# Sample keys turned by VectorE in 32x32 blocks, and sample scores in 16 tiles of the PE array, in a hybrid decoder layer

## The chip, the cores and the metric

The kernel runs on one core of a Trainium2 chip. Its five engines are TensorE (PE, with its weight loads PEld), VectorE (DVE), ScalarE (ACT), GpSimd (POOL) and SyncE (SP, here only a queue for DMAs). The metric is the time of one execution on the device in microseconds (us). Less is better.

## The reference, cut to what matters

One decoder layer takes a prompt of 256 tokens and 8 sample requests of 8 tokens each (64 sample rows, so 320 token columns). One projection `w_in` makes q, k, v, gates, indexer inputs and pool inputs for all of them, and `w_out` mixes the two branches back. The change touches one step of branch A, the attention of the sample requests. Each request has 8 pages of 128 cached keys and values, found through a page table, and 8 new keys:

```python
k_sel = jnp.where(in_past, cache_k[phys, row], gather_rows(k_new, ns).astype(cache_k.dtype))
qg = q.reshape(B, T, N_KV_HEADS, R, D)
logits = jnp.einsum('btgrd,btkgd->btgrk', qg, k_sel, preferred_element_type=F32) * (D ** -0.5)
bias = rel_bias[bucket].astype(F32).reshape(B, T, K, N_KV_HEADS, R)
logits = logits + jnp.transpose(bias, (0, 1, 3, 4, 2))
p = jax.nn.softmax(logits, axis=-1)
o = jnp.einsum('btgrk,btkgd->btgrd', p.astype(v_sel.dtype), v_sel)
```

There are 16 heads in 4 key groups of width 128. The kernel doesn't gather the chosen keys: it scores all 1032 keys of a request (1024 cached, 8 new) and adds a mask that leaves the chosen ones. A request's queries are 128 columns, 32 for each key group.

## The kernel before, in words

The program is a chain of segments over the columns of the projections: `qi`, `qkv`, `q`, `u`, `gb`, `ga`, `out`. Each takes its weights in chunks of 4 x 128 rows by 256 columns (512 KB). For each chunk SP issues the load (`load_chunk`), ACT copies it rounded into `hi` (`hi_chunk`), DVE makes the rest `lo` (`lo_chunk`), and PE runs 24 products of 320 columns each (`products`). There are four slots: ACT may write the slot of chunk c once PE has used chunk c - 4, and ACT and DVE work three chunks ahead of PE. Sixteen chunks are a quad, and after each half of a quad DVE empties two PSUM banks.

The other work is woven between the chunks. In the segment `ga` (4 quads, 64 chunks) it is the sample attention: request `b` takes 8 chunks, and `s` counts them. `pe_weave`, `act_weave` and `dve_weave` give what each engine does after its chunk `s`:

- s = 1 and 2: PE turns the 8 key pages in 32 transposes of 128x128 (L1397) into PSUM; ACT and DVE copy four pages each into `KTs` (`turned_keys`, L1444 and L1438). At s = 2 DVE copies the 8 new keys and the request's queries `qb` (L1465, L1466); ahead of the copies it waits for `e_in`, the load of all sample queries `qS` from DRAM, which ACT issues at the start of the segment (L1845).
- s = 3: PE computes the scores in 12 matmuls (L1406), each of 128 rows by 32 columns of the array, with up to 512 keys moving; `e_s` says that they are done. DVE adds bias and mask (L1470), adds the scaled scores (L1473) and takes the maximum (L1475).
- s = 4: ACT takes the exponential (L1447). s = 5: PE turns the weights of the keys (9 transposes, L1413), ACT copies them.
- s = 6: PE multiplies with the values (36 matmuls, L1423), DVE scales the result into `oN` (L1483). s = 7: PE turns `oN` (L1429), ACT stores it in `qS`.

In a weave the engine's own chunk work stands first: what DVE does after its chunk j comes behind `lo_chunk` of chunk j + 3, and all engines take their instructions in the order written.

GpSimd issues the page loads in its own queue (`on_gpsimd`, L1768). For each further request `b` it waits until the key pages of the one before are turned (`e_kt`), loads 8 key pages of 256 KB (`load_pages`, a page-table read and a DMA each), waits for the transposes of s = 5 and loads the mask, waits for the values' matmuls and loads 8 value pages. The first request's keys are loaded much earlier (`ahead`), the first mask and values at the start of the segment.

## Time and profile before

| | |
|---|---|
| time, median of 3 runs | 2105.53 us (2102.64 to 2108.89) |
| the profiled execution's own time | 2103.51 us |
| its span | 2101.9 us |
| PE busy | 2085.8 us (99% of the span) |
| DVE busy | 1165.2 us (55%) |
| ACT busy | 743.4 us (35%) |
| POOL busy | 409.2 us (19%) |
| mean DMA rate | 193 GB/s |

The page splits the span into 40 slices; PE stands at 9 tenths in all but the last, and the granted TensorE clock at full speed. The segment `ga` lies from about 1324 us to 1623 us of the span, where slices 26 to 32 show the highest DMA rates (240 to 256 GB/s). Times in the rows are microseconds from the span's start. An fp32 matmul of the program appears as two instructions: the 12 score matmuls of a request are 24 in its row.

### The profile page before, as it was taken

The page shows a single profiled execution, that of the slowest core. Times are in us where ns is not written, and L with a number is a line of the kernel's source. Part 1 is how long each engine was busy: PE and PEld are TensorE (multiplying, and loading weights), DVE is VectorE, ACT ScalarE, POOL GpSimd, SP SyncE. Part 2 cuts the span into 40 slices and gives each one's busy share as a digit, 9 for nine tenths or more (in the row PEclk, how much of TensorE's full clock was granted, in tenths as well). Part 3 has the DMA queues.
Part 4 walks back from the last instruction along what each step waited for, and adds up shares of the span by engine and source line. Part 5 has one row for each costly group of instructions (what it writes and reads, how often), then busy time and mean ns, then how long its engine had stood idle before and what let it go on. Part 6 is the DMA issues. An engine that isn't in the chain of part 4 may idle for free. (4 is left out here: it accounts for less than half of the span.)

```text
span 2101.9 us, 38946 instructions
## 1 busy us (share of the span) xinstructions
PE 2085.8 (99%) x14337; PEld 1991.3 (95%) x14337; DVE 1165.2 (55%) x1409; ACT 743.4 (35%) x925; POOL 409.2 (19%) x574
## 2 busy tenths in 40 slices
PE   9999999999999999999999999999999999999997
PEld 7888888999999999999999999999999999999997
DVE  5544544455555445566776767565665744444444
ACT  6433333323332333333333323333334433333333
POOL 1101000011110010235642102222222411111100
PEclk9999999999999999999999999999999999999999
DMA  8777776755554565666666657878787755555454
GB/s 232 210 220 212 224 205 204 221 153 160 147 164 127 179 191 173 181 194 170 196 199 194 189 152 220 255 241 256 244 255 250 240 166 161 163 164 160 152 156 145
DMA packets 341328, 406.01 MB, mean 193 GB/s; under 512 B 20332, under 2 KB 316204, under 8 KB 341000
## 3 DMA queue, kind: packets, MB, share of 16 engines
q1 hardware_dynamic: 293704, 291.75, 47.6%
q0 software_dynamic: 29968, 94.61, 14.5%
q10 hardware_dynamic: 17584, 18.70, 2.7%
q8 instruction: 44, 0.72, 0.1%
q14 instruction: 28, 0.23, 0.0%
HBM read 377.68 MB, written 31.45 MB: 195 GB/s over the span
## 5 line engine op out<-in xcount | busy, mean ns | idle before, releaser
L245 DVE TENSOR_TENSOR lo<-raw,hi 128x1024 fp32r<-128x1024 f32 x542 | 693.3, 1283 | 665.9 <-ACT hi L240 665.6
L269 PE MATMUL bank<-XX,hi 128*128 128x320 f32 x3264 | 1029.1, 315 | 0.2 <-DVE XX L1619 0.2
L271 PE MATMUL bank<-XX,lo 128*128 128x320 f32 x3264 | 1008.7, 309 | 0.0
L270 PE MATMUL bank<-XX,hi 128*128 128x320 f32 x3264 | 1008.3, 309 | 0.0
L240 ACT ACTIVATE hi<-raw 128x1024 fp32r<-128x1024 f32 x542 | 569.9, 1057 | 866.4 <-PE bank L271 533.9
L269 PEld LDWEIGHTS bank<-XX,hi 128*128 128x128 f32 x3264 | 613.0, 188 | 8.9 <-issue 5.0
L270 PEld LDWEIGHTS bank<-XX,hi 128*128 128x128 f32 x3264 | 613.2, 188 | 2.1
L271 PEld LDWEIGHTS bank<-XX,lo 128*128 128x128 f32 x3264 | 612.6, 188 | 0.0
L256 PE MATMUL bank<-XX,hi 128*128 128x512 f32 x1024 | 355.9, 392 | 0.0
L257 PE MATMUL bank<-XX,lo 128*128 128x256 f32 x1024 | 286.8, 280 | 0.0
L256 PEld LDWEIGHTS bank<-XX,hi 128*128 128x128 f32 x1024 | 191.5, 187 | 42.5 <-issue 0.2
L257 PEld LDWEIGHTS bank<-XX,lo 128*128 128x128 f32 x1024 | 193.5, 189 | 0.0
L1829 POOL TENSOR_TENSOR ends<-ends 128x512 f32 (+1 forms) x16 | 26.1, 1648 | 352.4 <-ACT ends L1571 334.8
L540 POOL DMA_DIRECT2D biasP<-biasD x16 | 8.6, 537 | 272.0 <-PE bank L257 272.0
L824 ACT ACTIVATE relu<-wide 128x384 f32<-128x384 f32 (+1 forms) x32 | 14.0, 438 | 119.5 <-PE wide L786 86.4
L377 DVE TENSOR_TENSOR stg<-bank,rstdB 128x320 f32<-128x320 f32 x72 | 32.0, 486 | 40.0 <-PE bank L271 40.0
L729 POOL DMA_DIRECT2D ipg<-cache_idx_k x64 | 34.7, 542 | 99.6 <-issue 99.6
L1758 POOL DMA_DIRECT2D deck<-cache_k x64 | 34.5, 539 | 92.9 <-issue 92.9
L1072 POOL DMA_DIRECT2D oT<-ohT x16 | 8.8, 551 | 184.8 <-ACT ohT L1266 184.1
L1306 DVE MAX8 tops<-scS 64x8 f32<-64x1032 f32 x32 | 39.1, 1222 | 0.0
L1308 DVE MATCH_REPLACE8 scS<-tops,scS 64x1032 f32<-64x1032 f32 x32 | 38.7, 1209 | 0.0
L1238 PE MATMUL wide<-dl,wp 128*128 128x320 f32 x128 | 37.0, 432 | 0.0
(298 smaller groups left out, 1534.1 us busy)
## 6 DMA issues: line engine op xcount, KB each, us to landing
raw<-w_in SPq DMA_DIRECT2D x416, 512.0 KB, 3.9
raw<-w_out SPq DMA_DIRECT2D x128, 512.0 KB, 3.7
deck<-cache_k POOLq DMA_DIRECT2D x64, 256.0 KB, 4.4
projT<-stg ACTq DMA_DIRECT2D x35, 320.0 KB, 2.9
keep<-cache_v POOLq DMA_DIRECT2D x40, 256.0 KB, 3.5
deck<-cache_v POOLq DMA_DIRECT2D x24, 256.0 KB, 3.7
deck<-maskD POOLq DMA_DIRECT2D x8, 516.0 KB, 5.7
ipg<-cache_idx_k POOLq DMA_DIRECT2D x64, 64.0 KB, 2.6
```

What stands on the lines that cost most here:

```text
L240: nc.scalar.activation(dst, raw[:, slot, :, 0:width], ACT.Copy).then_inc(hi_ready, 1)
L245: nc.vector.tensor_tensor(low, raw[:, slot, :, 0:width], high.bitcast(F32), ALU.subtract).then_inc(lo_ready, 1)
L256: nc.tensor.matmul(both, wh, XX[:, k, :, FREE:N], start=first, stop=False)
L257: mm = nc.tensor.matmul(bank[banks[n]][:, LATE:2 * LATE], wl, XX[:, k, 0, FREE:N], start=False, stop=last)
L269: nc.tensor.matmul(sums, wh, XH[:, k, :], start=first, stop=False)
L270: nc.tensor.matmul(sums, wh, XL[:, k, :], start=False, stop=False)
L271: mm = nc.tensor.matmul(sums, wl, XH[:, k, :], start=False, stop=last)
L729: pool.dma_start(ipg[:, p, :], tile_rows(t["cache_idx_k"][0], page)).then_inc(s_ipg, 16)
L1238: mm = nc.tensor.matmul(sbank[3][:, 0:N], wp[:, a, dt * P:(dt + 1) * P], dl[:, a, :], start=a == 0, stop=a == 3)
L1306: nc.vector.max(tops[:], scS[:]).then_inc(ts_step, 1)
L1308: nc.vector.match_replace(scS[:], tops[:], scS[:], TAKEN).then_inc(ts_step, 1)
L1758: pool.dma_start(dst[p], tile_rows(src, page)).then_inc(landed, 16)
```

## The change

Key pages. A page is now loaded in rows of 32: its 128 keys lie in 32 partitions with 4 keys in each. Two pages share a quarter of the partitions, so the same 2 MB fill the same buffer in another arrangement. DVE turns each of the 8 slots of that buffer with one 32x32-block transpose of 128 x 512 elements (`turned_pages`) straight into `KX`. The 32 transposes on PE and the 8 copies by ACT and DVE are gone. DVE turns the pages of request b + 1 in three shares, during s = 4, 5 and 6 of request b, and those of request 0 after the first three chunks of the segment. The first share waits for all 8 pages.

Scores. They come from 64 matmuls on 32 rows by 32 columns of the array with 256 keys moving, 16 tiles of the array in turn, each summed over four pieces of the head width, and 4 small matmuls for the new keys. Each row tile writes its own PSUM bank, and DVE adds the scores in two instructions instead of one.

Queries. Every row tile needs the queries of its 32 rows of the head width in its own partitions, so `qb` goes to DRAM once (`store_q`, 64 KB) and is read back four times into `qB` (`load_q`, 4 DMAs of 64 KB). GpSimd issues these: `store_q` after the first four key pages, `load_q` after the last four, ahead of the mask. `store_q` waits for `e_kn`, the copy of the queries, which DVE now makes at s = 4 of the request before (`new_keys`). For request 0 the copies and their wait for `e_in` stand after the first chunk.

```diff
             def pe_weave(pe, q, j):
                 u, s = j // 8, j % 8
                 b = q * BQ + u
-                if s in (1, 2):
-                    for p in range(4 * s - 4, 4 * s):
...
-                        for g in range(G):
-                            tr = nc.tensor.transpose(sbank[p % 4][:, g * P:(g + 1) * P], kpg[:, p, g * P:(g + 1) * P], ident[:])
-                        tr.then_inc(e_kt, 1)
                 if s == 3:
...
+                    pe.wait_ge(e_ptA, b)
+                    pe.wait_ge(e_o, b)
                     pe.wait_ge(e_kn, b * 2 + 2)
-                    for c in range(0, LS, 512):
-                        z = min(LS, c + 512)
-                        for g in range(G):
-                            mm = nc.tensor.matmul(wide[32 * g:32 * g + 32, c:z], qb[:, 32 * g:32 * g + 32], KTs[:, g, c:z],
-                                                  start=True, stop=True, skip_group_check=True)
+                    pe.wait_ge(e_kt, b * PAGES + PAGES)
+                    pe.wait_ge(e_qB, b * 64 + 64)
+                    alone(pe)
+                    for c in range(4):
+                        for a in range(4):
+                            for g in range(G):
+                                rows, quarter = slice(32 * a, 32 * a + 32), slice(32 * g, 32 * g + 32)
+                                nc.tensor.matmul(sbank[a][quarter, 0:PAST // 4], qB[rows, c, quarter],
+                                                 KX[rows, 4 * g + c, :, :].rearrange("p n k -> p (n k)"),
+                                                 start=c == 0, stop=c == 3, skip_group_check=True)
+                    for g in range(G):
+                        quarter = slice(32 * g, 32 * g + 32)
+                        mm = nc.tensor.matmul(sbank[0][quarter, PAST // 4:PAST // 4 + T_S], qb[:, quarter], KN[:, g, :],
+                                              start=True, stop=True, skip_group_check=True)
                     mm.then_inc(e_s, 1)
...
+            def turned_pages(dve, b, pages):
+
+                for p in pages:
+                    if p == 0:
+                        dve.wait_ge(e_k, b * (16 * PAGES) + 16 * PAGES)
+                        dve.wait_ge(e_s, b)
...
+                    nc.vector.transpose(KX[:, :, p, :], kpg[:, p, :].rearrange("p (b k) -> p b k", k=32)).then_inc(e_kt, 1)
+
+            def new_keys(dve, b):
+                dve.wait_ge(e_s, b)
+                nc.vector.tensor_copy(KN, kT[:, :, ds(b * T_S + T_P, T_S)]).then_inc(e_kn, 1)
+                nc.vector.tensor_copy(qb.rearrange("p (h n) -> p h n", h=H), qS[:, :, ds(b * T_S, T_S)]).then_inc(e_kn, 1)
...
+            SHARES = (range(0, 3), range(3, 6), range(6, PAGES))
+
+            def dve_weave(dve, q, j, first=False, last=False):
...
+                if first and j < 3:
+                    if j == 0:
+                        dve.wait_ge(e_in, 16)
+                        new_keys(dve, 0)
+                    turned_pages(dve, 0, SHARES[j])
+                if s == 4 and not (last and u):
+                    new_keys(dve, b + 1)
+                if s in (4, 5, 6) and not (last and u):
+                    turned_pages(dve, b + 1, SHARES[s - 4])
...
+                    if dst is keys:
+                        rows = rows.rearrange("(j k) n -> k j n", k=32)
+                    pool.dma_start(dst[p], rows).then_inc(landed, 16)
+
+            keys = [kpg[16 * (p - p % 2):16 * (p - p % 2) + 32, 4 * (p % 2):4 * (p % 2) + 4, :] for p in range(PAGES)]
...
+                def store_q(b):
+                    pool.wait_ge(e_kn, b * 2 + 2)
+                    alone(pool)
+                    pool.dma_start(tile_rows(qD, b), qb).then_inc(e_qD, 16)
+
+                def load_q(b):
+                    pool.wait_ge(e_qD, b * 16 + 16)
+                    alone(pool)
+                    for a in range(4):
+                        src = qD[ds(b, 1)].rearrange("o (c p) n -> p (o c) n", p=32)
+                        pool.dma_start(qB[32 * a:32 * a + 32, :, :], src).then_inc(e_qB, 16)
...
                 load_mask(0)
-                load_pages(pool, 0, "cache_v", vpg, e_v, PAGES // 2)
+                store_q(0)
+                load_pages(pool, 0, "cache_v", vpg, e_v, PAGES // 2, PAGES - 2)
+                load_q(0)
+                load_pages(pool, 0, "cache_v", vpg, e_v, PAGES - 2)
                 load_vnew(0)
                 with pool.Fori(1, NB_S) as b:
                     pool.wait_ge(e_kt, b * PAGES)
                     alone(pool)
-                    load_pages(pool, b, "cache_k", keys, e_k)
+                    load_pages(pool, b, "cache_k", keys, e_k, 0, PAGES // 2)
+                    store_q(b)
+                    load_pages(pool, b, "cache_k", keys, e_k, PAGES // 2)
+                    load_q(b)
                     pool.wait_ge(e_pt, b)
                     alone(pool)
                     load_mask(b)
```

On DVE, in one request of the segment. In the rows `lo` is the chunk work, `deck` holds the logits and keys, `wide` is PSUM and `keep` holds queries and `oN`. Before, from the new keys of a request to its `oN`:

```order
L1465 COPY deck<-keep 128x4x8
L1466 COPY keep<-keep 128x128
L245 TENSOR_TENSOR lo<-raw,hi 128x1024
L1470 TENSOR_TENSOR deck<-deck 128x1032
L1473 SCALAR_TENSOR_TENSOR deck<-wide,deck 128x1032
L1475 TENSOR_REDUCE st<-deck 128x1
L245 TENSOR_TENSOR lo<-raw,hi 128x1024 x2
L1478 RECIPROCAL st<-st 128x1
L245 TENSOR_TENSOR lo<-raw,hi 128x1024
L1483 TENSOR_SCALAR keep<-wide,st 128x128
```

Now, from the maximum of a request to its `oN`:

```order
L1487 TENSOR_REDUCE st<-deck 128x1
L246 TENSOR_TENSOR lo<-raw,hi 128x1024
L1442 COPY deck<-keep 128x32
L1443 COPY keep<-keep 128x128
L1438 STREAM_TRANSPOSE deck<-deck 128x16x32 x3
L246 TENSOR_TENSOR lo<-raw,hi 128x1024
L1438 STREAM_TRANSPOSE deck<-deck 128x16x32 x3
L1490 RECIPROCAL st<-st 128x1
L246 TENSOR_TENSOR lo<-raw,hi 128x1024
L1438 STREAM_TRANSPOSE deck<-deck 128x16x32 x2
L1495 TENSOR_SCALAR keep<-wide,st 128x128
```

The copies for the next request and its eight transposes now stand between the maximum and the `oN` of this one.

On GpSimd, at the end of a request's key pages in the loop (`deck<-cache_k` is a key page, `keep<-cache_v` a value page, an ISA row is a wait or a register move). Before:

```order
L1757 TENSOR_LOAD ptab
L1757 ISA x2
L1758 ISA
L1758 DMA deck<-cache_k 128x512
L1771 ISA
L1771 DMA deck<-maskD 128x1x1032
L1757 TENSOR_LOAD ptab
L1757 ISA x2
L1758 ISA
L1758 DMA keep<-cache_v 128x512
```

Now, at the fourth page, and then behind the eighth:

```order
L1773 DMA deck<-cache_k 32x4x512
L1789 ISA
L1791 ISA
L1791 DMA qD<-keep 128x128
L1769 ISA
L1769 TENSOR_LOAD ptab
L1769 ISA x2
L1773 ISA
L1773 DMA deck<-cache_k 32x4x512
...
L1794 ISA
L1798 DMA keep<-qD 32x4x128 x4
L1786 ISA
L1786 DMA deck<-maskD 128x1x1032
```

The store of the queries, with its wait, stands in the middle of the key pages, and four loads stand ahead of the mask.

## Rows read from the trace of the kernel before

**Rows 1.** Windows view: us; PE, PEld, DVE, ACT, POOL busy (instructions); clock, DMA share, GB/s.

```profile
1420.00:1457.00 37.00, 37.00 (x330) 34.96 (x329) 22.37 (x24) 13.77 (x18) 9.29 (x18) 1.00 0.77 248
```

**Rows 2.** Timeline of PE, one request, product rows between: start us, us, instructions.

```profile
1369.85 1.91 PE L1397 MATMUL wide<-ident,deck 128*128 128x128 f32 x16
1371.51 0.39 PE L269 MATMUL bank<-XX,hi 128*128 128x320 f32 x1
...
1382.38 0.41 PE L269 MATMUL bank<-XX,hi 128*128 128x320 f32 x1
...
1394.12 1.30 PE L1423 MATMUL wide<-keep,deck 128*32 128x128 f32 x40
...
1396.35 0.41 PE L269 MATMUL bank<-XX,hi 128*128 128x320 f32 x1
1399.97 0.27 PE L1429 MATMUL wide<-ident,keep 128*128 128x128 f32 x1
...
1417.86 1.97 PE L1406 MATMUL wide<-deck,keep 128*32 128x512 f32 x24
1426.90 1.14 PE L1413 MATMUL wide<-ident,deck 128*128 128x128 f32 x9
```

**Rows 3.** Timeline of DVE in the same stretch.

```profile
1396.55 0.35 DVE L1483 TENSOR_SCALAR keep<-wide,st 128x128 f32<-128x128 f32 x1 [2.46 <-PE wide L1423]
...
1412.14 1.28 DVE L1438 COPY deck<-wide 128x512 f32<-128x512 f32 x2
...
1419.99 1.23 DVE L1473 SCALAR_TENSOR_TENSOR deck<-wide,deck 128x1032 f32<-128x1032 f32 x1 [1.74 <-PE wide L1406]
1421.26 1.23 DVE L1475 TENSOR_REDUCE st<-deck 128x1 f32<-128x1032 f32 x1
1422.40 1.22 DVE L245 TENSOR_TENSOR lo<-raw,hi 128x1024 fp32r<-128x1024 f32 x1
```

**Rows 4.** Timeline of GpSimd in the same stretch.

```profile
1417.14 0.54 POOL L1758 DMA_DIRECT2D deck<-cache_k  x1 [0.79 <-issue]
1418.38 0.54 POOL L1758 DMA_DIRECT2D deck<-cache_k  x1 [0.70 <-issue]
...
1428.79 0.54 POOL L1771 DMA_DIRECT2D deck<-maskD  x1 [3.70 <-PE wide L1413]
```

**Rows 5.** DMA issues (count, KB each, median us to landing): segment ga, then whole span.

```profile
deck<-cache_k POOLq DMA_DIRECT2D x48, 256.0 KB, 4.2
...
oT<-ohT POOLq DMA_DIRECT2D x16, 128.0 KB, 2.2
keep<-projT ACTq DMA_DIRECT2D x1, 512.0 KB, 10.1
```

**Rows 6.** All page loads of L1758: time to landing, min/median/max.

```profile
DMA to landing us min/median/max: 2.8/4.1/7.8
```

**Rows 7.** Timelines of ACT, DVE and PE in the first request.

```profile
1332.50 0.41 ACTq L1845 DMA_DIRECT2D keep<-projT  x1
...
1334.27 2.36 DVE L245 TENSOR_TENSOR lo<-raw,hi 128x1024 fp32r<-128x1024 f32 x2 [2.57 <-ACT hi L240]
...
1342.78 0.18 DVE L1465 COPY deck<-keep 128x32 f32 x1 [2.62 <-DMA keep<-projT]
1342.92 0.23 DVE L1466 COPY keep<-keep 128x128 f32 x1
...
1343.20 1.97 PE L1406 MATMUL wide<-deck,keep 128*32 128x512 f32 x24 [0.87 <-DVE keep L1466]
...
1345.10 0.41 PE L269 MATMUL bank<-XX,hi 128*128 128x320 f32 x1
```

**Rows 8.** Windows view at the span's start and end, and PE's last busy window.

```profile
15.00:20.00 5.00, 5.00 (x32) 4.63 (x32) 1.61 (x4) 2.28 (x6) 2.10 (x4) 0.81 1.04 332
...
2091.00:2094.00 3.00, 0.89 (x8) 0.63 (x6) 1.17 (x5) 0.80 (x3) 0.00 (x0) 1.00 0.57 222
2094.00:2096.00 2.00, 0.00 (x0) 0.00 (x0) 1.95 (x5) 1.16 (x2) 0.00 (x0) 0.90 0.03 7
```

More of the change, by code:

```diff
@@ L112, in hybrid_layer @@
     maskD = dram("maskD", (N_S, LS))
+    qD = dram("qD", (NB_S, P, H * T_S))
     biasD = dram("biasD", (H, VEC))
@@ L154, in hybrid_layer @@
         ptab = sb("ptab", [1, NB_S * PAGES], I32)
-        keep = sb("keep", [P, G * N + (LS + 1) // 2 + L2 + L2 // 2 + 3 * KVW + POOLW // P * NB_S * STATE])
+        keep = sb("keep", [P, G * N + 4 * H * T_S + L2 + L2 // 2 + 3 * KVW + POOLW // P * NB_S * STATE])
         at = [0]
@@ L423, in hybrid_layer @@
         gated_a, exped_a = sem("gated_a"), sem("exped_a")
-        (e_in, e_rel, e_k, e_v, e_mask, e_masked, e_vnew, e_kt, e_kcA, e_kcD, e_kn, e_s, e_lg, e_mx, e_exp, e_ri, e_pt,
+        (e_in, e_rel, e_k, e_v, e_mask, e_masked, e_vnew, e_kt, e_qD, e_qB, e_kn, e_s, e_lg, e_mx, e_exp, e_ri, e_pt,
          e_ptA, e_pv, e_on, e_ot, e_o) = (sem(n) for n in (
-             "e_in", "e_rel", "e_k", "e_v", "e_mask", "e_masked", "e_vnew", "e_kt", "e_kcA", "e_kcD", "e_kn", "e_s", "e_lg",
+             "e_in", "e_rel", "e_k", "e_v", "e_mask", "e_masked", "e_vnew", "e_kt", "e_qD", "e_qB", "e_kn", "e_s", "e_lg",
              "e_mx", "e_exp", "e_ri", "e_pt", "e_ptA", "e_pv", "e_on", "e_ot", "e_o"))
@@ L1429, in pe_weave @@
                     nc.tensor.transpose(sbank[3][:, P:2 * P], oN, ident[:]).then_inc(e_ot, 1)
-            def turned_keys(eng, copy, s, b, even, done):
-                eng.wait_ge(e_s, b)
-                eng.wait_ge(w_pe, 4 * NG)
-                eng.wait_ge(ut_out, 16 * NG * (NB_S + 1))
-                for p in range(4 * s - 4 + (0 if even else 1), 4 * s, 2):
-                    eng.wait_ge(e_kt, b * PAGES + (p + 1))
-                    copy(KTs[:, :, p * P:(p + 1) * P], sbank[p % 4].rearrange("p (g n) -> p g n", g=G)).then_inc(done, 1)
+            def turned_pages(dve, b, pages):
[3 more added lines that the diff above has]
+                        dve.wait_ge(e_s, b)
+                        dve.wait_ge(w_pe, 4 * NG)
+                        dve.wait_ge(ut_out, 16 * NG * (NB_S + 1))
+                    nc.vector.transpose(KX[:, :, p, :], kpg[:, p, :].rearrange("p (b k) -> p b k", k=32)).then_inc(e_kt, 1)
[3 more added lines that the diff above has]
+                nc.vector.tensor_copy(qb.rearrange("p (h n) -> p h n", h=H), qS[:, :, ds(b * T_S, T_S)]).then_inc(e_kn, 1)
             def act_weave(act, q, j):
@@ L1442, in act_weave @@
                 b = q * BQ + u
-                if s in (1, 2):
-                    turned_keys(act, lambda o, i: nc.scalar.activation(o, i, ACT.Copy), s, b, True, e_kcA)
                 if s == 4:
@@ L1757, in load_pages @@
                     page = pool.value_load(ptab[0:1, ds(b * PAGES + p, 1)], min_val=0, max_val=N_PHYS - 1)
-                    pool.dma_start(dst[p], tile_rows(src, page)).then_inc(landed, 16)
-            keys = [kpg[:, p, :] for p in range(PAGES)]
+                    rows = tile_rows(src, page)
+                    if dst is keys:
+                        rows = rows.rearrange("(j k) n -> k j n", k=32)
+                    pool.dma_start(dst[p], rows).then_inc(landed, 16)
+            keys = [kpg[16 * (p - p % 2):16 * (p - p % 2) + 32, 4 * (p % 2):4 * (p % 2) + 4, :] for p in range(PAGES)]
             def ahead(pool):
@@ L1860, in on_vector @@
             def on_vector(dve):
-                with dve.Fori(0, NQ - 1) as q:
+                dve_quad(dve, "ga", 0, lambda eng, q, j: dve_weave(eng, q, j, first=True), gate=gate)
+                with dve.Fori(1, NQ - 1) as q:
                     dve_quad(dve, "ga", q, dve_weave, gate=gate)
-                dve_quad(dve, "ga", NQ - 1, then_mix(dve_weave, dve_mix), gate=gate, open_end=True)
+                dve_quad(dve, "ga", NQ - 1, then_mix(lambda eng, q, j: dve_weave(eng, q, j, last=True), dve_mix), gate=gate,
+                         open_end=True)
                 dve_quad(dve, "out", 0, mix_weave(dve_mix, dve_gating), turned=f_t, first=True)
```

39 lines of the change are left out of this document (14 added, 25 removed).

## The prediction, made before the changed kernel ran

> **What bounds the kernel now.** I read the busy shares first, then the windows of the segment `ga`, where the change sits. A window as long as one request has PE busy in all of its 37.00 us at full clock, and DVE in 22.37 [rows 1]. So PE sets the pace here, and what the change takes from PE is a gain as long as nobody makes PE wait. Next comes PE's timeline, to see where a request's time goes. From the first score matmul of one request to that of the next there are 37.4 us: the scores give way to products at 1382.38, `oN` is turned 17.6 us later at 1399.97, and the next scores start at 1417.86, 17.9 us after that; the scores themselves take 1.9 us (1343.20 to 1345.10) [rows 2, 7]. Last I read the timelines of DVE and GpSimd, for what each does between the scores and `oN` [rows 3, 4], since the order puts new work there.
>
> **PE: what goes and what comes.** Sixteen transposes take 1.66 us (1369.85 to 1371.51) [rows 2]; a request has two such sets, so 3.3 us go. The 17.9 us from `oN` to the next scores become 14.6.
>
> The scores are new in form, and no row shows row tiles at work. Before, 24 instructions (two for each of 12 fp32 matmuls) took 1.9 us. Now there are 136. The multiplications are the same: 16 tiles of 32x32 fill the array as the four of 128x32 did. If the array is the limit, they take 1.9 us again. But each instruction is only 256 columns long and shares the array with 15 others. The nearest row in count is the product with the values: 36 matmuls, 72 instructions, from 1394.12 to 1396.35, which is 2.23 us or 31 ns each [rows 2]. At that rate 128 instructions take 4.0 us. The upper end is that row tiles don't overlap: four times the array time, 4 x 1.7 = 6.8 us. I take 3.8, near the row of 31 ns. So PE alone would need 37.4 - 3.3 - 1.9 + 3.8 = 36.0 us for a request, a gain of 1.4 us.
>
> [...]
>
> **The loop through DVE and GpSimd.** This is the part that decides. I count from the moment when the scores of request b end (1419.76 in the stretch of [rows 2 to 4], since they started at 1417.86), as time 0.
>
> - DVE adds scores at 0.23, for 1.23 us; a second small add, 0.2; then the maximum, 1.23; then `lo` of a chunk, which adds 1.15 (starts 1422.40, ends 1423.62, overlapping a little) [rows 3]. That is 4.0.
> - DVE copies the new keys and queries of request b + 1: 0.37 us (1342.78 to 1343.15) [rows 7]. That is 4.4, and only now does `e_kn` let GpSimd go on.
> - GpSimd stands at `store_q`, with four key pages still to issue behind it. Between a release and its DMA lie 0.75 us (PE's transposes end at 1428.04, the mask's DMA starts at 1428.79) [rows 2, 4]. The store starts at 5.15 and ends at 5.69. The first page follows after 0.70, and pages follow each other by 1.24 (1417.14, 1418.38) [rows 4]. So the eighth page is issued at 6.4 + 3 x 1.24 = 10.1.
> - It lands 4.2 us later [rows 5], at 14.3. All key pages lie between 2.8 and 7.8 [rows 6]. Before, this landing had most of a request to happen in. Now DVE waits for it in its queue, with two more `lo`, five more transposes and `oN` behind it.
> - Eight block transposes of 512 elements. No row shows one. Two copies of the same size from PSUM take 1.28 us [rows 3], so 0.6 each from start to start. A cheaper end is 0.4, the dearer end is twice the copy, 1.2. I take 0.6.
> - Three transposes 1.9, `lo` 1.15, a reciprocal 0.15, three transposes 1.8, `lo` 1.15, two transposes 1.25, `oN` 0.35: 7.75 us. So `oN` is there at 22.1.
>
> [...]
>
> PE reaches its wait for `oN` at 17.6. It stands still for 4.5 us. The chunk that PE needs next was made lo at 17.4, so this is one wait and not two. Then come 14.6 us and the scores, 3.8: the period is 22.1 + 14.6 + 3.8 = 40.5 us against 37.4. Seven periods lie between the scores of the first and the last request: 7 x 3.1 = +22 us. Behind the last request nothing is turned, and PE's way to the end is as before.
>
> Everything else that is off PE is covered while the loop holds. ACT's four copies go and were hidden. DVE loses four copies of 0.6 and gets eight transposes of 0.6, within 14 us of idle time per request [rows 1]. The four loads of `load_q` follow the key pages and are wanted some 20 us later; the mask behind them has until the next scores.
>
> **The first request.** In `new_keys` of request 0 DVE waits for `e_in` after the first chunk, with `lo` of the next chunk behind it. ACT issues that load at 1332.50 and it takes 10.1 us; DVE could copy at 1342.78. It had been idle for 2.6 us then, with its other work done [rows 5, 7]. Now DVE stands from 1335.5 on. Meanwhile GpSimd stands at `store_q` too, so fewer pages compete with this load: I let it land at 1339.5 (ends: 1337, 1342.6). Then: copies 1340, store issued 1341, two value pages to 1343.7, four loads of queries to 1346, landing 3.5 to 4.2 later, 1349.7. The pages are turned by 1347.3 (8 x 0.6, two `lo`, copies). PE comes at 1339 and waits for 10 us. The scores end near 1349.7 + 3.8 + 1.7 = 1355, where the 1.7 is the clock, below. Before, products followed at 1345.10 [rows 7]. That is +10 us.
>
> **The clock.** At the end of the span PE is last busy between 2091 and 2094 and the clock is at its lower level for a fifth of 2094 to 2096 (mean 0.90), so it fell near 2095.6, after less than 4 us of idleness or so. At the start, PE was busy in all of 15 to 20, yet the mean is 0.81: 1.9 of 5 us at the lower level [rows 8]. [...] I put in 1 us on each of 7 waits: +7.
>
> **Sum.** 2103.5 (the profiled execution) + 10 + 22 + 7 = 2142.5. That execution is 2 us under the median of the runs, so beside them 2143.
>
> **The rivals.**
> - The loop closes in time, PE keeps the bound. For it: landings as short as 2.8, transposes at 0.4, together 3 us less in the chain, and scores at the array's limit. Then the wait is 1.5 us without a change of clock, the period 35.6 (19.1 + 14.6 + 1.9), seven times -1.8, with +6 at the start: 2097. Against it: three good ends at once. With transposes and landings good and the scores at 2.7 the period is 36.4, and the time about 2103.5 - 7 + 7 = 2104. The faster side starts where `oN` comes before 19.5 and the scores take under 2.5 us. Chance 0.08 for the faster end, 0.05 for the case that comes out as no change.
> - Row tiles don't overlap: the scores take 6.8 us. For it: no row shows the overlap. Eight times +3: 2167. Chance 0.12. If nothing overlapped at all, 64 x 0.43 = 27 us each, 2330; chance 0.02.
> - Block transposes cost 1.2 us. Then +4.8 in each chain, seven times, plus 3: 2180. Chance 0.08.
> - Weights run late. DMA share is 0.77 and 248 GB/s in the segment [rows 1]. Against it: a longer period lowers the rate. As the whole effect it would have PE waiting for `lo` and not for `oN`. It adds 5 to 15 us in 0.05.
> - Forecast: the loop. Chance 0.60.
>
> A difference under 0.3%, 6 us, can't be told from none. Slower 0.87, within 0.05, faster 0.08. The range for 8 in 10 is 2112 to 2175: the lower end is landings of 2.8, transposes of 0.5 and scores near 3, the upper end the rows of tiles that don't overlap with the clock low after each wait.
>
> **What would show it.** Right: after the scores of requests 0 to 6, DVE's first transpose idle for 8 to 10 us on a DMA of `cache_k`; the first of these about 14 us after the scores; PE's L1428 idle for 3 to 6 us on DVE; a clock under 1.00 in these windows; PE's scores near 3.8 us; in the first request DVE's copy idle on `keep<-projT` and PE's first score matmul idle for about 10 us. Wrong: PE busy in all of a request's window (then PE kept the bound), score bursts of 1.9 or 6.8 us, or transposes far from 0.6 us. If the last four key pages were issued before the copy of the queries, the whole loop would be misread.

## The result and the profile after

The changed kernel takes 2161.48 us (median of four runs, 2159.49 to 2163.63) against 2107.21 for the kernel before (2102.64 to 2109.61) on the same chip. The ratio is 1.0261, with a 95% interval of 1.0240 to 1.0281: slower. The forecast was 2143 us with a range of 2112 to 2175. The direction and the range held, and 18 us were missing from the sum. For the profiled execution by itself the sum was 2142.5 and 2163.63 us came out: 21.1 missing.

Two rows of the profile page after, the queue of instructions (packets, MB, share) and the costliest groups:

```profile
q8 instruction: 65, 1.06, 0.2%
...
L1438 DVE STREAM_TRANSPOSE deck<-deck 128x512 f32<-128x512 f32 x64 | 40.7, 683 | 71.4 <-DMA deck<-cache_k 71.4
```

DVE waits 71.4 us for key pages ahead of its new transposes. And the queue that the page calls "instruction" moved 65 packets, which I read as code brought to the engines. The page of before has 44 there. That difference belongs to a third of the loss, as the experiments show.

PE's waits inside `ga` (1320 to 1700 us), as us in total, times, longest:

```profile
PE wide L1428 <- DVE keep L1495: 28.3, 7, 4.9
PE wide L1400 <- DMA keep<-qD: 12.0, 1, 12.0
PE bank L270 <- issue: 11.4, 2, 5.8
PE bank L271 <- issue: 8.4, 2, 5.1
```

The first row is the loop through DVE and GpSimd, in seven of the eight requests. The second is the first request. The other two were in no part of the forecast: PE stands at a product (L270, then L271) for which nothing that the profile shows had to be waited for.

Windows of three successive requests, each from one end of scores to the next, then short windows around two of the waits (columns as in [rows 1]):

```profile
1396.30:1447.10 50.80, 37.58 (x416) 35.28 (x411) 24.75 (x29) 11.57 (x14) 12.74 (x23) 0.87 0.64 194
1447.10:1489.10 42.00, 37.98 (x416) 35.54 (x411) 24.33 (x29) 11.46 (x14) 12.71 (x23) 0.92 0.81 226
1489.10:1542.00 52.90, 38.19 (x411) 35.89 (x411) 24.76 (x29) 11.57 (x14) 12.59 (x23) 0.84 0.64 186
1418.00:1424.00 6.00, 0.33 (x1) 0.14 (x1) 5.16 (x7) 0.90 (x2) 2.73 (x5) 0.58 1.05 345
...
1468.00:1473.00 5.00, 4.68 (x18) 4.68 (x19) 3.09 (x6) 1.85 (x3) 2.14 (x4) 0.50 1.01 357
```

A request was 37.00 us of busy PE at clock 1.00 in [rows 1]. Now most requests take 41 to 42 us, and two take 50.8 and 52.9. The last row is the stretch right after a wait of 3.5 us: PE is busy in 4.68 of 5 us, and the granted clock is 0.50. That is the lower of the two levels, 1.00 and 0.50, at which the clock stands in all the traces here; a mean between them is a window that holds both.

PE's timeline shows where the long requests differ from the others:

```profile
1351.16 4.00 PE L1400 MATMUL wide<-deck,keep 32*32 32x256 f32 x128 [11.98 <-DMA keep<-qD]
...
1418.44 0.33 PE L1428 MATMUL wide<-ident,keep 128*128 128x128 f32 x1 [4.41 <-DVE keep L1495]
...
1424.35 0.63 PE L270 MATMUL bank<-XX,hi 128*128 128x320 f32 x1 [5.58 <-issue]
...
1428.21 0.42 PE L271 MATMUL bank<-XX,hi 128*128 128x320 f32 x1 [3.23 <-issue]
...
1444.20 2.76 PE L1400 MATMUL wide<-deck,keep 32*32 32x256 f32 x128
1446.89 0.25 PE L1405 MATMUL wide<-deck,keep 128*32 128x8 f32 x8
...
1468.32 0.47 PE L1428 MATMUL wide<-ident,keep 128*128 128x128 f32 x1 [3.49 <-DVE keep L1495]
...
1516.65 0.63 PE L270 MATMUL bank<-XX,hi 128*128 128x320 f32 x1 [5.78 <-issue]
...
1522.43 0.43 PE L271 MATMUL bank<-XX,hi 128*128 128x320 f32 x1 [5.15 <-issue]
```

Both "issue" pairs stand at the first products of a quad, where the loop over quads on PE jumps back. Four quads make the segment, and the loop body is the code of one quad with its two requests. It jumps back twice, into the second and the third quad; the last one is written out behind the loop.

The same request on DVE, answering to [rows 3]:

```profile
1447.28 1.22 DVE L1483 SCALAR_TENSOR_TENSOR deck<-wide,deck 128x1024 f32<-128x1024 f32 x1 [3.03 <-PE wide L1405]
...
1450.97 0.22 DVE L1443 COPY keep<-keep 128x128 f32 x1
...
1460.84 1.90 DVE L1438 STREAM_TRANSPOSE deck<-deck 128x512 f32<-128x512 f32 x3 [9.64 <-DMA deck<-cache_k]
...
1467.96 0.31 DVE L1495 TENSOR_SCALAR keep<-wide,st 128x128 f32<-128x128 f32 x1
```

And on GpSimd, answering to [rows 4]:

```profile
1452.01 0.56 POOL L1791 DMA_DIRECT2D qD<-keep  x1 [24.05 <-DVE keep L1443]
...
1457.12 0.55 POOL L1773 DMA_DIRECT2D deck<-cache_k  x1 [0.72 <-issue]
```

The chain is the one of the forecast. The scores end at 1447.14. DVE copies the queries at 1450.97, GpSimd issues the store at 1452.01 after standing for 24.05 us, and the eighth page follows at 1457.12. DVE's first transpose begins at 1460.84, 13.7 us after the scores (forecast 14.3). `oN` is ready 21.1 us after them, and PE turns it at 21.2 (forecast 22.1).

**The account.** The profiled spans differ by 2162.1 - 2101.9 = 60.2 us. The first request gives 10.2 of it (its scores end at 1355.3 instead of 1345.1). The seven periods between ends of scores were 41.0, 50.8, 42.0, 52.9, 41.1, 42.0 and 41.2. The seven before run from 1343.20 [rows 7] to the start of the last request's scores:

```profile
1604.22 1.97 PE L1406 MATMUL wide<-deck,keep 128*32 128x512 f32 x24
```

That is 261.0 us, or 37.3 (37.29) each; the 37.4 of [rows 2] was the longest. The five periods without a jump have a mean of 41.46, which is 4.17 more: 7 x 4.17 = 29.2. The two with a jump have 9.3 and 11.4 on top: 20.7. Together that is 60.1.

### The profile page after: what moved, and what is told of

The parts are those of the page before. It is cut to its first block and busy times, and to the rows that moved or that the text cites. A ratio compares the mean times of both kernels' runs of the same rounds, so it can differ in the third digit from the quotient of the medians.

```text
span 2162.1 us, 40238 instructions
## 1 busy us (share of the span) xinstructions
PE 2084.9 (96%) x14977; PEld 1989.6 (92%) x14977; DVE 1181.3 (55%) x1449; ACT 726.2 (34%) x893; POOL 433.5 (20%) x614
## 5 line engine op out<-in xcount | busy, mean ns | idle before, releaser
L270 PE MATMUL bank<-XX,hi 128*128 128x320 f32 x3264 | 1035.1, 317 | 12.3 <-issue 11.4
L271 PE MATMUL bank<-XX,hi 128*128 128x320 f32 x3264 | 1014.7, 311 | 8.4 <-issue 8.4
L270 PEld LDWEIGHTS bank<-XX,hi 128*128 128x128 f32 x3264 | 619.1, 190 | 21.8 <-issue 16.8
L271 PEld LDWEIGHTS bank<-XX,hi 128*128 128x128 f32 x3264 | 619.1, 190 | 2.1
L1438 DVE STREAM_TRANSPOSE deck<-deck 128x512 f32<-128x512 f32 x64 | 40.7, 683 | 71.4 <-DMA deck<-cache_k 71.4
L730 POOL DMA_DIRECT2D ipg<-cache_idx_k x64 | 34.7, 542 | 99.6 <-issue 99.6
```

The lines of the kernel that those rows point to most:

```text
L270: nc.tensor.matmul(sums, wh, XH[:, k, :], start=first, stop=False)
L271: nc.tensor.matmul(sums, wh, XL[:, k, :], start=False, stop=False)
L730: pool.dma_start(ipg[:, p, :], tile_rows(t["cache_idx_k"][0], page)).then_inc(s_ipg, 16)
L1438: nc.vector.transpose(KX[:, :, p, :], kpg[:, p, :].rearrange("p (b k) -> p b k", k=32)).then_inc(e_kt, 1)
```

## The experiments

The question was what the two gaps at the jumps are, and whether the loop through DVE is really what the other waits come from. My first theory made one thing of both: PE waits for `oN`, its queue of instructions runs dry meanwhile, and the fetch of the next code lies open. The rival was that the two are independent, and that the code of a quad had become too long. The first four kernels ran together (before: 2108.19 us).

### All key pages ahead of the store of the queries

```
                     alone(pool)
-                    load_pages(pool, b, "cache_k", keys, e_k, 0, PAGES // 2)
+                    load_pages(pool, b, "cache_k", keys, e_k)
                     store_q(b)
-                    load_pages(pool, b, "cache_k", keys, e_k, PAGES // 2)
                     load_q(b)
```

> The changed kernel, but GpSimd issues all eight key pages of a request ahead of the store and the loads of the queries. Theory (a loop: queries copied, then four key pages issued and landed, then DVE goes on to oN, then PE): the pages are there long before DVE wants them, DVE's idle time on cache_k (71 us now) goes to under 5, PE's wait for oN (28 us) goes, and with it the two gaps of PE at the first product of a quad (20 us, put down to the fetch of instructions that only an empty PE queue lets show). A period of 37.4 - 3.3 - 1.9 + 2.95 = 35.1 us, the first request's +8 to +10 stays: 2103.5 + 10 - 7 x 2.3 = 2097 us (2092 to 2104). Rival (the pages in 32 partitions land late by themselves, 5.5 us median now): PE still waits in each request, over 2120. Rival (the two gaps are late weights and have nothing to do with the wait): the waits go and the gaps stay, about 2118.

Measured: 2129.81 us (2125.96 to 2131.83), ratio 1.0108 (1.0083 to 1.0132), 31.7 under the changed kernel, but far from the 2097 that I expected. PE's waits in `ga`:

```profile
PE bank L270 <- issue: 14.1, 2, 7.4
...
PE bank L271 <- issue: 7.8, 2, 4.0
PE wide L1428 <- DVE keep L1495: 2.3, 3, 1.0
```

Moving four pages ahead of one store takes the wait for `oN` from 28.3 to 2.3 us. So the place of the store in GpSimd's queue did cause those waits. The gaps at the jumps stay, and with 21.9 us they are no smaller than before. The timeline shows them without a wait for `oN` ahead of them:

```profile
1410.46 0.31 PE L1428 MATMUL wide<-ident,keep 128*128 128x128 f32 x1
...
1418.16 0.63 PE L270 MATMUL bank<-XX,hi 128*128 128x320 f32 x1 [7.40 <-issue]
...
1422.59 0.42 PE L271 MATMUL bank<-XX,hi 128*128 128x320 f32 x1 [3.80 <-issue]
...
1438.21 2.75 PE L1400 MATMUL wide<-deck,keep 32*32 32x256 f32 x128
...
1472.93 2.46 PE L1400 MATMUL wide<-deck,keep 32*32 32x256 f32 x110
```

The last two rows give an undisturbed period: 34.7 us, against 37.3 before. So PE's own saving is real: 2.6 us per request.

### PE's quads written out instead of looped over

```
             def on_tensor(pe):
-                with pe.Fori(0, NQ - 1) as q:
+                for q in range(NQ - 1):
                     pe_quad(pe, "ga", q, pe_weave)
```

> The changed kernel, but PE's first three quads of the segment ga are written out instead of a loop with two jumps back; all other engines as they are. Theory (the gaps of 5.6 + 3.2 us and 5.8 + 5.1 us at a quad's first products are PE's instructions coming late after the jump back, which shows only since PE's queue is empty behind the wait for oN): the two long periods (51.6 and 54.0 us between score starts) fall to the 41 to 42 of the others, 2161.5 - 23 = 2138 us (2130 to 2146). Rival (late weights, or the gate work of DVE and ACT at the end of a quad): they stay, 2161.

Measured: 2140.38 us (2136.47 to 2144.16), ratio 1.0165 (1.0142 to 1.0189), 21.1 under the changed kernel. PE's waits in `ga`:

```profile
PE wide L1428 <- DVE keep L1495: 27.7, 7, 4.5
```

The reverse picture: the wait for `oN` stays in all seven places, and the gaps at the jumps are gone. The 21.1 us agree with the 20.7 of the account, and the time with the 2138 expected. Its page still counts 59 instruction packets, 15 more than before, but PE stands behind one of them only once in `ga`, for 1.0 us (its scores go on at 1397.40, 1.3 us after a packet that ended at 1396.10).

### The kernel before, with `oN` made late

Three groups of VectorE operations on data that nothing reads afterwards stand ahead of `oN` in the first six requests.

```
                     dve.wait_ge(e_ot, b)
+                    for p, n in ((1, G), (3, G), (5, 2)):
+                        nc.vector.reciprocal(KTs[:, 0:n, p * P:(p + 1) * P], KTs[:, 0:n, p * P:(p + 1) * P])
                     nc.vector.tensor_scalar(oN, sbank[3][:, 0:HD], ...).then_inc(e_on, 1)
```

> The kernel before, with 8.3 us of extra work for DVE (reciprocals of 512, 512 and 256 columns of key copies that nothing reads any more) ahead of oN in the first six requests, which makes oN late. It lies on both sides of PE's two jumps back. Theory (a wait just ahead of the jump makes the fetch show): oN comes at 14.2 + 8.3 = 22.5 us after the scores instead of 14.2, where PE comes at 17.6: six waits of 5 us, half a us to a us each for the clock, and gaps of 8 to 11 us of PE behind the jumps, which the kernel before doesn't have: 2103.5 + 6 x 5.5 + 20 = 2157 us (2145 to 2165). Rival (the gaps come from something else in the changed kernel, its DMAs or its longer program): no gaps, 2103.5 + 33 = 2137.

Measured: 2148.07 us (2145.11 to 2153.90), ratio 1.0205 (1.0180 to 1.0230), between the two times expected. PE's timeline:

```profile
1386.45 1.97 PE L1406 MATMUL wide<-deck,keep 128*32 128x512 f32 x24
...
1410.91 0.47 PE L1429 MATMUL wide<-ident,keep 128*128 128x128 f32 x1 [4.81 <-DVE keep L1486]
...
1431.06 1.97 PE L1406 MATMUL wide<-deck,keep 128*32 128x512 f32 x24
...
1475.36 1.97 PE L1406 MATMUL wide<-deck,keep 128*32 128x512 f32 x24
```

The period with a jump is 44.6 us, the next one 44.3: no gap, although the waits are as long as in the changed kernel. With the kernel above, where the gap stands without the wait, this ends my first theory: a wait is neither needed nor enough. It also prices a wait. Each of the six periods is 7.0 to 7.3 us longer than the same one before. Of that 4.8 is standing still, and 2.2 to 2.5 is what follows: the clock stands at 0.50 for 6.8 us each time (1408.7 to 1415.5 around the wait shown).

### The pages turned later on VectorE

```
-                if s in (4, 5, 6) and not (last and u):
-                    turned_pages(dve, b + 1, SHARES[s - 4])
+                if s == 7 and not (last and u):
+                    turned_pages(dve, b + 1, SHARES[0])
+                if s in (0, 1) and not (first and j < 8):
+                    turned_pages(dve, b, SHARES[s + 1])
```

> The changed kernel with GpSimd's order as it is (the store of the queries in the middle of the key pages), but DVE turns the pages of request b + 1 in s = 7 of request b and s = 0 and 1 of its own, behind oN, as before. Theory (what hurts is that oN stands behind the landing of the pages in DVE's queue, not the landing itself): the pages land at 14 us after the scores and DVE comes to them at about 15, so hardly a wait, PE has none for oN, no gaps: 2097 us (2092 to 2106), as with the keys first. Rival (the late issue or slow landing hurts by itself): PE waits for e_kt or weights, over 2110.

Measured: 2129.02 us (2127.03 to 2129.62), ratio 1.0104 (1.0082 to 1.0125). DVE's waits for key pages fall from 71.4 to 4.3 us and PE's for `oN` are gone. The gaps stay, which the 2097 expected did not have:

```profile
1414.70 0.63 PE L270 MATMUL bank<-XX,hi 128*128 128x320 f32 x1 [6.29 <-issue]
...
1420.76 0.43 PE L271 MATMUL bank<-XX,hi 128*128 128x320 f32 x1 [5.42 <-issue]
```

So the loop can be cut on DVE as well as on GpSimd, for the same 32 us. That is what a chain through both would have.

### The kernel before, with a longer body

If the length of the code is the cause, the kernel before must show gaps once its body is as long. Per quad, PE issues 1320 weight loads and matmuls before, and 1640 after the change. Forty more matmuls of 8 columns, each two instructions and two weight loads, bring a request from 660 to 820.

```
+                    for _ in range(10):
+                        for g in range(G):
+                            mm = nc.tensor.matmul(wide[32 * g:32 * g + 32, PAST:LS],
+                                                  qb[:, 32 * g:32 * g + 32], KTs[:, g, PAST:LS],
+                                                  start=True, stop=True, skip_group_check=True)
                     mm.then_inc(e_s, 1)
```

> The kernel before with 40 more matmuls of 8 columns behind each request's scores (each two weight loads and two matmuls), which write the same values again. PE's loop over a quad grows from 1320 weight loads and matmuls to 1640, as long as the changed kernel's. Theory (the gaps come when the body of PE's loop is too long to be still at hand after the jump back): two gaps of 8 to 13 us appear at the first products of the second and third quad, with 20 more instruction packets, and each request is 1.5 to 2.5 us longer: 2108 + 16 + 22 = 2146 us (2136 to 2155). Rival (the gaps need something of the changed kernel's, its row tiles, its DMAs): no gaps, 2124.

Measured: 2128.63 us (2127.28 to 2131.51), ratio 1.0110 (1.0092 to 1.0128), beside a kernel before of 2106.52. PE's timeline at the jump:

```profile
1407.66 0.41 PE L269 MATMUL bank<-XX,hi 128*128 128x320 f32 x1 [1.16 <-issue]
...
1412.08 0.43 PE L270 MATMUL bank<-XX,hi 128*128 128x320 f32 x1 [4.01 <-issue]
```

The gaps appear, at the same place, in a kernel with nothing else of the change, and its page counts 65 instruction packets as after the change. The trace also has the time of each packet. Between 1410 and 1550 us, while PE goes round the loop, this kernel and then the changed one show

```profile
q8 instruction: 14, 0.23, 0.6%
q8 instruction: 14, 0.23, 0.7%
```

and the kernel before shows none in that stretch. The packets also stand where the gaps are. Here one ends at 1405.96 and PE's first product starts at 1407.66; the next ends at 1410.78 and the second product starts at 1412.08. In the changed kernel the ends are 1422.67 and 1426.72, the products start at 1424.35 and 1428.21. So each gap ends 1.3 to 1.7 us after a packet of instructions has come. Periods without a jump are 38.0 us, those with one 45.3 and 44.5. With gaps of 5.2 and 4.9 us, against 8.8 and 10.9 after the change, the 2146 expected was too high.

### Half of that addition

The same edit with `range(5)` gives a body of 1480.

> The same with 20 more matmuls for each request: a body of 1480 weight loads and matmuls. It halves the interval in which the bound lies. If the body of 1480 is still at hand: 2108 + 8 = 2116 us with 44 instruction packets in all. If not: gaps, 2138 with some 60.

Measured: 2108.83 us (2106.89 to 2114.43, 8 runs), ratio 1.0014 (1.0000 to 1.0028). A jump costs at most 0.1 us (37.76 and 37.65 us against 37.65 in the other periods), the added matmuls cost 0.4 us per request and not the 1 expected, and the instruction queue is back at

```profile
q8 instruction: 45, 0.74, 0.1%
```

No packet of that queue falls between 1410 and 1550 us. So a body of 1480 went round the loop without a new packet, and one of 1640 brought 14 in that stretch. What happens between the two lengths wasn't measured.

### A shorter body in the changed kernel

The kernel with all key pages first, with `for c in range(2)` in the scores: half of the head width is left out, and the body falls to 1384.

> The changed kernel with the keys first, and two of the four pieces of the head width left out of the scores (the sum is over 64 of 128). PE's loop has 1384 weight loads and matmuls instead of 1640. Theory (length of the body): the two gaps (7.4 + 3.8 and 6.7 + 4.0 us with the keys first) are gone or under 2 us, and the scores take half: 2130 - 22 - 8 x 1.4 - 2 (clock) = 2095 us. Rival (the gaps come from late weights or pages after the jump): the gaps stay, 2118. For the scores: at the issue rate seen now (2.75 us for 128 instructions, 21.5 ns each) 64 instructions take 1.4 us.

Measured: 2100.99 us (2098.39 to 2102.58, 7 runs), ratio 0.9977 (0.9963 to 0.9990), 6 us above the 2095 expected. Of the 11 us that stood at the first jump, this is left:

```profile
1411.88 0.41 PE L270 MATMUL bank<-XX,hi 128*128 128x320 f32 x1 [0.15 <-issue]
```

No instruction packet falls between 1410 and 1550 us. The change's own code shows no gap either once it is short enough. (Its time is no gain of the change, since half the scores' work is missing.)

### Key pages first and PE written out

Both edits of above, that of GpSimd's order and that of PE's loop, in one kernel.

> The changed kernel with only two changes of order: all key pages ahead of the query store in GpSimd's queue, and PE's first three quads written out instead of the loop. It asks whether the two causes add up and what is left. Keys first alone gave 2130, written out alone 2140, the changed kernel 2161. Theory (they are separate): against keys first the two gaps go, with the slow clock behind each, 2 x 11 us: 2130 - 22 + 3 for bubbles in dense stretches = 2111 us (2105 to 2116). What is left against the kernel before is the first request, +10, less the gain per request. Rival (one cause seen twice): 2125 or more.

Measured: 2115.88 us (2111.68 to 2120.88, 10 runs) beside 2105.32 before, ratio 1.0043 (1.0026 to 1.0059). The two edits give 31.7 and 21.1 us alone and 45.6 together, so they are two causes, with 7 us less than the sum. PE's waits in `ga`:

```profile
PE wide L1428 <- DVE keep L1495: 3.3, 2, 2.6
PE bank L271 <- issue: 2.4, 1, 2.4
...
PE wide L1405 <- issue: 2.0, 1, 2.0
```

The first request costs 10.7 us here. The seven periods after it take 256.8 us together, 4.2 less than before, where 34.7 each would have given 18 less. These waits and the lower clock behind two of them (3.4 us at that level each time) take most of the rest. So the saving on PE is mostly lost even without the jumps. Both "issue" waits end 1.4 us after an instruction packet (1395.29 and 1540.89), as at the jumps.

### The way through DRAM replaced by copies on ACT

To take the first request as well, 16 ACT copies of 32 partitions hold the queries four times, in place of the store and the four loads. In request 0 the pages are turned ahead of the wait for `e_in`. Key pages come first and PE is written out.

```
+            def held_four_times(act, b):
+                act.wait_ge(e_kn, b * 2 + 2)
+                for a in range(4):
+                    for c in range(4):
+                        copy = nc.scalar.activation(qB[32 * a:32 * a + 32, c, :],
+                                                    qb[32 * c:32 * c + 32, :], ACT.Copy)
+                copy.then_inc(e_qB, 1)
...
-                store_q(0)
-                load_pages(pool, 0, "cache_v", vpg, e_v, PAGES // 2, PAGES - 2)
-                load_q(0)
-                load_pages(pool, 0, "cache_v", vpg, e_v, PAGES - 2)
+                load_pages(pool, 0, "cache_v", vpg, e_v, PAGES // 2)
```

> The changed kernel with three edits: all key pages ahead in GpSimd's order, the queries held four times by 16 copies of 32 partitions on ACT instead of the way over DRAM (for the first request after s = 2, with DVE turning its pages ahead of the wait for e_in), and PE's first three quads written out. Theory: the period is 34.8 us as between the jumps with the keys first, seven times -2.7 against the kernel before (37.5); no gaps; the first request's scores wait for e_in (1341), two copies and 16 short ACT copies (4 us), so they start at 1346 instead of 1343, and end 4 us later than before: 2108 - 19 + 4 + 1 = 2094 us (2088 to 2100), ratio 0.993. Rival (copies between partition quarters are slow on ACT or hold up hi): over 2108.

Measured: 2108.51 us (2104.91 to 2115.45, 12 runs), ratio 1.0021 (1.0009 to 1.0033), not the 2094 that I expected. PE's timeline:

```profile
1349.19 4.52 PE L1400 MATMUL wide<-deck,keep 32*32 32x256 f32 x128 [9.94 <-ACT keep L1449]
...
1574.24 0.66 PE L1400 MATMUL wide<-deck,keep 32*32 32x256 f32 x14 [2.44 <-issue]
```

The first request still costs 8.8 us (its scores end at 1353.9): `e_in` now landed at 1343.5, and 16 copies of 0.31 us come behind it. In straight code PE stands 1.3 to 2.4 us in three places. From 1326 to 1606 us the DMA share is 0.92, against 0.82 before. Of the kernels that compute everything with the change in them, this is the fastest, and it is no faster than before.

### The copies divided, and the scores in two halves

The same with 12 copies on DVE and 4 on ACT, the pages turned later, and the scores issued in two halves.

```
+                split = not (isinstance(q, int) and q == 0 and u == 0)
...
+                if s in (2, 3):
+                    for c in (((0, 1), (2, 3)) if split else ((), range(4)))[s - 2]:
```

> The best that the runs so far point to: keys first, PE's quads written out, the queries held four times by copies (12 on DVE, 4 on ACT, 0.15 and 0.31 us each) instead of the way over DRAM, pages turned in s = 7, 0 and 1, and the scores in two halves after s = 2 and s = 3, so that PE's short instructions come less densely. Theory: against the kernel with ACT copies (2108.5) the first request's scores start at 1345.5 instead of 1349.2 (-3.5), DVE's and PE's waits on pages go (-2), and the 5.5 us that PE lacked instructions in dense stretches fall to 2 (-3): 2100 us (2094 to 2106), ratio 0.997. Rival (the DMA engines, at a share of 0.95 in these requests, are the next bound): weights come late instead, 2106 to 2110.

Measured: 2131.92 us (2126.51 to 2135.87), ratio 1.0122 (1.0101 to 1.0143): a miss, as 2100 was expected and 2110 at most. PE's waits in `ga`:

```profile
PE wide L1403 <- DVE deck L1442: 16.1, 3, 5.6
PE wide L1403 <- DVE keep L1451: 10.1, 1, 10.1
PE wide L1403 <- issue: 9.7, 4, 2.5
```

The scores one step earlier ask for pages that DVE, with 12 copies of 0.22 us more, hasn't turned yet. The copies hold up the first request. The four "issue" waits stand at the start of the scores and end 6 to 14 us after the last instruction packet, so they are not the gaps of above; what they are stays open.

### What the burst of scores is made of

Two kernels with key pages first tell how 128 instructions share the array. In one only 128 of the 256 columns are computed:

```
-  nc.tensor.matmul(sbank[a][quarter, 0:PAST // 4], qB[rows, c, quarter], KX[rows, 4 * g + c, :, :]...
+  nc.tensor.matmul(sbank[a][quarter, 0:PAST // 8], qB[rows, c, quarter], KX[rows, 4 * g + c, 0:4, :]...
```

> The changed kernel with the keys first, and each of the 64 score matmuls over 128 keys instead of 256 (half of the keys are left out of the scores). It measures what sets the 2.75 us of a score burst of 128 instructions (21.5 ns each). If the pace of instructions sets it: 2.6 to 2.75 us still. If the array does (16 tiles at once would need 13.3 ns each at 256 columns, 6.7 at 128): half, 1.4 us. If row tiles overlap only in part, in between.

In the other the loops over columns and rows of tiles change places:

```
-                        for a in range(4):
-                            for g in range(G):
+                        for g in range(G):
+                            for a in range(4):
```

> The changed kernel with the keys first, and the score matmuls in another order: the four row tiles (and with them the four PSUM banks) change fastest, the four column tiles slower. If the pace of instructions sets the burst: 2.75 us as before. If four following matmuls on the same rows and bank hold each other up, it becomes shorter, towards 1.9; if following matmuls on the same columns do, longer.

PE's timeline with half the columns (2129.45 us, one run):

```profile
1439.20 1.90 PE L1400 MATMUL wide<-deck,keep 32*32 32x128 f32 x128
1441.03 0.25 PE L1405 MATMUL wide<-deck,keep 128*32 128x8 f32 x8
```

and with the loops changed over (2127.68 us, one run, the kernel before beside both at 2105.01):

```profile
1436.95 2.76 PE L1400 MATMUL wide<-deck,keep 32*32 32x256 f32 x128
1439.64 0.25 PE L1405 MATMUL wide<-deck,keep 128*32 128x8 f32 x8
```

From the first start to the start of L1405 it is 1.83 us or 14.3 ns per instruction with 128 columns, and 2.69 us or 21.0 ns with 256. So 128 columns cost 6.7 ns. The kernel before says what columns take in one of the two instructions of an fp32 matmul. Of the 24 instructions in its first request [rows 7] 16 have 512 columns, and narrow windows show them in groups of four, one on each column tile:

```profile
1343.20 0.64 PE L1406 MATMUL wide<-deck,keep 128*32 128x512 f32 x4 [0.87 <-DVE keep L1466]
...
1343.66 0.61 PE L1406 MATMUL wide<-deck,keep 128*32 128x512 f32 x4
...
1344.09 0.61 PE L1406 MATMUL wide<-deck,keep 128*32 128x512 f32 x4
...
1344.51 0.61 PE L1406 MATMUL wide<-deck,keep 128*32 128x512 f32 x4
```

The groups follow each other by 0.43 us (the first by 0.46), and four of them are 1.7 us, under the 1.9 us with the eight short ones in it. A quarter of the columns, 128, is an estimated 0.43 / 4 = 0.107 us, and shared by 16 tiles 6.7 ns. That is just what 128 columns cost here. So all 16 tiles overlap, rows as well as columns. What remains is constant: 21.0 - 13.4 = 7.6 ns per instruction, and 14.3 - 6.7 = 7.6 with half the columns. The order of the tiles changes nothing. Neither pure expectation, a cost by columns or a cost by instruction, was right: it is the sum of both, as far as two sizes, each from one run, can show it.

## Why the prediction was right in part

**The first request: right** (+10 forecast, +10.2 measured), by luck in its size. Two of its steps were off and cancelled: `e_in` landed at 1341.24 instead of 1339.5, and the scores took 4.2 us from 1351.16, with a mean clock of 0.64, instead of 3.8 + 1.7.

**The loop through DVE and GpSimd: right, and shown.** It was forecast as 22 us, with 7 for the clock beside it: 29, and 29.2 was measured. No run shows the 1 us that the sum has for the clock at each wait, nor the 1.7 of the first request; the runs showed the 1.6 to 2.8 us below at a wait, and in the first request scores of 4.2 us in all. Taking either the pages or the transposes out of the chain removes it. Inside, sizes were off and made up for each other, so that the number is as close as that is luck. A period was forecast as 22.1 us from the scores to `oN`, 14.6 and 1 for the clock to the next scores, and 3.8 for the scores: 41.5. The five without a jump have 21.7, 16.4 and 3.3 on average. At full clock the middle part takes 14.3 us (1458.65 to 1472.93 with the keys first). Here it took 15.9 to 17.1, so the lower clock cost 1.6 to 2.8 us and not 1; the kernel before with a late `oN` shows 2.2 to 2.5. The scores took 2.9 us with their small matmuls (2.69 without), and 3.7 and 4.0 in two requests with a short "issue" wait inside. The wait for `oN` was 4.0 us on average (28.3 over 7), not 4.5. The transposes were 0.63 us from start to start (three in 1.90), against 0.6.

**What failed: the sum has no term for PE's code.** In the change part by part I counted what the 136 instructions of the scores take on the array, and not what they do to the loop in which they stand. The first step of that was in front of me: "24 instructions ... Now there are 136". With their weight loads, less the transposes, a quad goes from 1320 to 1640, and at that length instruction packets come while PE goes round the loop (14 between 1410 and 1550 us, none before), and it stands at each jump back. Two jumps cost 20.7 us, nearly all of the 21.1 that the forecast for the profiled execution lacked. That the time stayed in the range is luck: its upper end was made for row tiles that don't overlap. The longer body alone in the kernel before makes the gaps and the 65 packets appear. A shorter body or written-out quads make them go. None of my rivals had this.

**The rival "row tiles don't overlap" is refuted**, by a burst of 2.70 us where it needed 6.8. The 1.7 us of array time behind that 6.8, and the 0.43 us behind the 27 us for all in a row, come from no row of the prediction, but the groups of four above show both: 1.7 us for the 16 long instructions, and 0.43 us for the columns of one matmul of 256, which is two instructions. Against the 27 us, 2.70 together is a factor of 10.

**The rival "PE keeps the bound"** needed the chain to close, and it does with key pages first: undisturbed requests then take 34.7 us. The time still stays above before, as the jumps and the first request cost more than seven times 2.6 us give back.

**Open.** I don't know why PE stands for 5 us at a jump in the lengthened kernel before and for 8.8 and 10.9 in the changed one. The packets narrow it down to when the fetch starts. At the first jump the lengthened kernel's packet starts at 1404.94, 1.6 us before PE has nothing left to do; in the changed kernel it starts at 1421.74, 3.0 us after, and with the keys first 4.6 us after. The DMA share in the window of the first gap was 1.00 in the changed kernel and 0.85 in the lengthened one, so the fetch may queue behind pages, but no run held the body and varied the traffic. For the length of the body at which the packets begin, the runs give only that it lies between 1480 and 1640. The clock's cost was read beside waits, never alone.

## What to carry to other kernels

When a change swaps few long instructions for many short ones, count the instructions of the loop body on that engine and compare the row of instruction packets in both profiles. The total alone doesn't decide (the written-out kernels have 59 and no long gap behind a packet), so look for packets in a window in which the loop runs. Here the idle times named "issue" at the first instructions after a jump back ended 1.3 to 1.8 us after an instruction packet, and writing the loop out or shortening it was the test. And when a store that waits for a late producer is put into an in-order DMA queue, everything behind it inherits that wait (here GpSimd stood for 24.05 us at the store of one request, with four key pages behind it): put the loads that others need ahead of it.

## What was new about the hardware

- A body of 1480 weight loads and matmuls on PE ran with at most 0.1 us more at the jump back (45 instruction packets), one of 1640 stood for about 5 us at each in one kernel and 8.8 to 11.7 in the changed one and its variants (65 packets). Straight code with dense short matmuls had gaps of 1.0 to 2.4 us. Gaps of both kinds ended 1.3 to 1.8 us after an instruction packet.
- In bursts of 32x32 tiles an fp32 instruction took the time of its columns over 16 tiles (an estimated 13.4 and 6.7 ns) plus 7.6 ns (21.0 ns with 256 columns, 14.3 with 128), the same with either tested order of the tiles.
- A block transpose of 128x512 fp32 on VectorE took 0.68 us (0.63 from start to start). An ACT copy of 32x128 took 0.31 us, a DVE copy 0.22 us.
- In the changed kernel each of the seven waits of 3.4 to 4.9 us on PE was followed by some us at a granted clock of 0.50 (3.4 to 6.8 us, and 13.7 and 17.1 where a jump came behind it). In the five requests without a jump that cost 1.6 to 2.8 us. Other waits did not follow their length: with the keys first and the quads written out two of 2.4 and 2.6 us were followed by it too, and with the quads alone written out one of 3.43 us was not (from it to the next scores 14.35 us went by, as at full clock).
